# Branch c's finish as a pipeline of tiles, its bonus operand made early, and the rounds' keys moved behind chain steps

## What is computed

```python
# six heads of 64 channels, two directions; t = 128 or 1024 tokens
S = S * w + (S @ -kk)[..., None] * (kk * a) + v[..., None] * k_dir      # the scan, with y = S @ r
k_dir = k[:, :, None, :] * (1 + (a - 1) * k_a)                          # per direction
y = head_norm(ys[0] + ys[1], ln_g, 6)                                   # mean and variance over 64 channels
bonus = sum over both directions and 64 channels of (r * k_dir * r_k)
y = (y + bonus * v) * g                                                 # g = sigmoid(dg) @ g2
```

## Time and profile before

| | |
|---|---|
| runs | 2104.83, 2108.36, 2111.37 us; median 2108.36 |
| profiled execution | 2114.14 us, its span 2112.4 us, mean granted TensorE clock 0.937 |
| PE, DVE, ACT, POOL busy | 1875.6, 1004.3, 601.9, 725.7 us |
| recurrence of branch c | about 656 to 1087 us of the span |
| finish of branch c | 1088.5 to 1179.3 us |

### The profile page before, as it was taken

How to read it: one execution, slowest core, us unless ns; L and a number is a source line. 1 busy time by engine, 2 the same in 40 slices (tenths; PEclk the granted TensorE clock), 3 DMA queues, 4 the chain that set the end, 5 groups by cost and what they waited for, 6 DMA issues and landing times. The chain is left out here.

```text
span 2112.4 us, 49389 instructions
## 1 busy us (share of the span) xinstructions
PE 1875.6 (89%) x20834; PEld 1755.2 (83%) x20834; DVE 1004.3 (48%) x1726; ACT 601.9 (28%) x1330; POOL 725.7 (34%) x559
## 2 busy tenths in 40 slices
PE   6599799998996888878754799999999999999998
PEld 3589798877996677767643699999999999999998
DVE  6603753767334455444458636333433343424254
ACT  4413243322125555445420224110101020201034
POOL 3502431444843222222220512443535344343460
PEclk7799898998998999899975799999999999999999
DMA  9555010111110000000010400120111111111122
GB/s 301 191 176 177 21 42 14 25 62 49 40 41 12 4 8 4 3 4 4 4 36 0 140 21 21 30 60 25 55 37 43 50 30 50 30 50 35 48 57 90
DMA packets 148180, 110.31 MB, mean 52 GB/s; under 512 B 13298, under 2 KB 144393, under 8 KB 147757
## 3 DMA queue, kind: packets, MB, share of 16 engines
q1 hardware_dynamic: 148013, 107.83, 16.8%
HBM read 93.17 MB, written 14.55 MB: 51 GB/s over the span
## 5 line engine op out<-in xcount | busy, mean ns | idle before, releaser
L253 PE MATMUL banks<-Z_r 128*128 128x384 f32 x2016 | 350.9, 334 | 0.0
L253 PEld LDWEIGHTS banks<-Z_r 128*128 128x128 f32 x2016 | 349.5, 188 | 0.4 <-issue 0.2
L2669 DVE SCALAR_TENSOR_TENSOR XT<-banks,MOD,XT 128x128 f32 x224 | 110.8, 516 | 226.1 <-PE banks L253 225.3
L3003 ACT ACTIVATE PAD<-banks 128x384 f32<-128x384 f32 x96 | 47.2, 491 | 504.3 <-PE banks L2898 504.1
L3119 DVE TENSOR_TENSOR PAD<-PAD 128x384 f32<-128x384 f32 x96 | 97.1, 1011 | 144.0 <-ACT PAD L3003 143.9
L235 POOL TENSOR_TENSOR Z_r<-Z,ones 128x512 fp32r<-128x512 f32 x56 | 77.0, 1375 | 253.9 <-DMA Z<-in_mlp_w 253.9
L235 POOL TENSOR_TENSOR W_r<-Z,ones 128x1024 fp32r<-128x1024 f32 x32 | 77.4, 2420 | 241.0 <-DMA Z<-in_mlp_w 240.9
L2898 PE MATMUL banks<-HT_r,W_r 128*128 128x384 f32 x768 | 149.1, 335 | 2.4 <-ACT HT_r L2970 1.6
L2898 PE MATMUL banks<-YT_r,W_r 128*128 128x384 f32 x768 | 148.6, 334 | 0.0
L2898 PE MATMUL banks<-HT_r,Z_r 128*128 128x384 f32 x768 | 148.6, 334 | 0.0
L2898 PEld LDWEIGHTS banks<-HT_r,W_r 128*128 128x128 f32 x768 | 134.4, 188 | 3.3 <-issue 1.9
(11 more groups left out here) (414 smaller groups left out, 4027.4 us busy)
## 6 DMA issues: line engine op xcount, KB each, us to landing
Z<-in_w_mod SPq DMA_DIRECT2D x16, 1024.0 KB, 5.1
Z<-in_mlp_w SPq DMA_DIRECT2D x32, 512.0 KB, 4.3
Z<-in_mlp_w SPq DMA_DIRECT2D x58, 256.0 KB, 2.8
YT<-in_w_in SPq DMA_DIRECT2D x18, 512.0 KB, 3.9
XT<-in_w_mod SPq DMA_DIRECT2D x8, 1024.0 KB, 9.0
residual<-Z SPq DMA_DIRECT2D x1, 4608.0 KB, 18.1
low_part<-XT_r SPq DMA_DIRECT2D x1, 4608.0 KB, 15.9
XT<-low_part SPq DMA_DIRECT2D x8, 576.0 KB, 5.5
```

The costliest lines, as they stand in the source:

```text
L253: mm = nc.tensor.matmul(self.bank(slot, g), w[slot][:, k, :], x(k, g), start=(n == 0 and k == 0), stop=(n == 2 and k == self.blocks - 1))
L2669: ins = nc.vector.scalar_tensor_tensor(out=x, in0=S.PS[3 * slot + g][:, a:b], scalar=S.MOD[:, ds(col, 1), c:c + 1].rearrange("p a b -> p ( ...
L3003: nc.scalar.activation(R[slot][:, grp(g)], up.bank(slot, g), ACT.Relu).then_inc(up.drained[g].sem, 1)
```

## The change

In the rounds: ACT copies q and u of the first half step before `ka_act`; DVE's `k_rows_dve` comes after the zero level's masks; POOL adds the unit matrix first, waits for the state of the first half step, and only then makes `k_dir` and the seeds; the state's multiplication is one instruction over both directions, for which the end decays of the backward direction are stored in reverse order. From round n = 5 on POOL makes the bonus operand of tiles whose keys are no longer needed, in place (in the gate sums and in rows 3 to 5 of Z), six instructions a tile, each followed by a wait for itself: tile 0, then two tiles a round.

In the finish, all written out without a loop: DVE centres tile t, multiplies v by the bonus of tile t - 1, reduces the squares of tile t and completes tile t - 2; ACT squares; POOL divides by the deviation (and does the weights' divisions behind tiles 1, 4 and 7); PE makes the gates for three tiles at a time in three banks, the bonus from the operand that is there, and the transposition. v is overwritten in place. The old body of `finish_c`, quoted above, goes.

```diff
@@ -2240,13 +2243,14 @@
     def round_act(act, chain, nxt, after, par):
         r, n, a = chain, nxt, after
+        if r is not None:
+            q_act(act, r, 0)
+            u_act(act, r, 0)
         if n is not None:
             tok = direction_tiles(act, n)[0]
             for d in range(2):
                 ka_act(act, n, d, tok[d])
         if r is not None:
-            q_act(act, r, 0)
-            u_act(act, r, 0)
             q_act(act, r, 1)
             u_act(act, r, 1)
         for d in range(2):
@@ -2313,10 +2317,9 @@
         heads = lambda x: x.rearrange("p d q n -> p (d q) n")
         nc.vector.tensor_tensor(heads(C.S), heads(C.S), by_block(bank(6)), ALU.add).then_inc(f["added"].sem, 1)
         done(dve, "added", r, j + 1)
-        for d in range(2):
-            ins = nc.vector.tensor_tensor(C.S[:, d, :, :], C.S[:, d, :, :],
-                                          C.ends[par][:, d, :, chunk(d, j)].unsqueeze(2).to_broadcast([P, NP, N]), ALU.mult)
-        ins.then_inc(f["new_state"].sem, 1)
+        ends = C.ends[par].rearrange("p d q j -> p (d q) j")[:, :, j]
+        nc.vector.tensor_tensor(heads(C.S), heads(C.S), ends.unsqueeze(2).to_broadcast([P, 2 * NP, N]),
+                                ALU.mult).then_inc(f["new_state"].sem, 1)
         if between:
             between()
         if j:
@@ -2362,8 +2365,6 @@
                 done(dve, "gram_l", n, d + 1)
                 nc.vector.tensor_tensor(C.LP[:, d, :, :, :].rearrange("p c q n -> p (c q) n"), by_block(bank(d)),
                                         mask(d, LEVELS, 2 * NP), ALU.mult).then_inc(f["masked_l"].sem, 1)
-            for d in range(2):
-                k_rows_dve(dve, n, d)
         if r is not None:
             state_dve(dve, r, par, 0, tiles, first if n is not None else None)
         elif n is not None:
@@ -2371,6 +2372,8 @@
         if n is not None:
             zm_dve(dve, n, 0, 0)
             zm_dve(dve, n, 0, 1)
+            for d in range(2):
+                k_rows_dve(dve, n, d)
         if r is not None:
             state_dve(dve, r, par, 1, tiles)
         if n is not None:
@@ -2408,19 +2411,37 @@
     def r_rows_pool(pool, a, d, par, tok):
         end = N if d == 0 else 0
         done(pool, "exped", a, d + 1)
-        nc.gpsimd.tensor_copy(C.ends[par][:, d, :, :], C.EP[:, d, :, :, end]).then_inc(f["ends"].sem, 1)
+        ends = C.EP[:, d, :, :, end]
+        nc.gpsimd.tensor_copy(C.ends[par][:, d, :, :], ends[:, :, ::-1] if d else ends).then_inc(f["ends"].sem, 1)
         for p in range(NP):
             ins = nc.gpsimd.tensor_tensor(tile_cols(C.RR[par][:, d, :, :], p),
                                           S.Z[:, p, ds(tok, P)].rearrange("p (c n) -> p c n", n=N),
                                           C.EP[:, d, p, :, own(d)], ALU.mult)
         ins.then_inc(f["r_rows"].sem, 1)
+    def bonus_pool(pool, t):
+        at = slice(t * P, (t + 1) * P)
+        both, keys = C.A[:, 0, :, at], S.Z[:, 3:6, at]
+        b = S.bonus_made
+        nonlocal n_bonus
+        def one(ins):
+            nonlocal n_bonus
+            n_bonus += 1
+            ins.then_inc(b.sem, 1)
+            pool.wait_ge(b.sem, b.at(0, n_bonus))
+        one(nc.gpsimd.tensor_tensor(both, both, C.A[:, 1, :, at], ALU.add))
+        for p in range(NP):
+            one(nc.gpsimd.tensor_scalar(both[:, p, :], both[:, p, :], C.bonus_scale[:, p:p + 1], C.bonus_shift[:, p:p + 1],
+                                        ALU.mult, ALU.add))
+        one(nc.gpsimd.tensor_tensor(keys, keys, both, ALU.mult))
+        one(nc.gpsimd.tensor_tensor(keys, keys, S.Z[:, 0:3, at], ALU.mult))
     def round_pool(pool, chain, nxt, after, par):
         r, n, a = chain, nxt, after
         if n is not None:
-            tok = direction_tiles(pool, n)[0]
-            for d in range(2):
-                k_dir_pool(pool, n, d, tok[d])
             for d in range(2):
                 done(pool, "masked_l", n, d + 1)
                 nc.gpsimd.tensor_tensor(C.LP[:, d, :, :, :].rearrange("p c q n -> p (c q) n"),
@@ -2429,6 +2450,12 @@
                                             f["unit_l"].sem, 1)
             before(pool, "tz", n)
             done(pool, "unit_l", n, 2)
+            if r is not None:
+                done(pool, "new_state", r, 1)
+            tok = direction_tiles(pool, n)[0]
+            for d in range(2):
+                k_dir_pool(pool, n, d, tok[d])
+            done(pool, "k_dir", n, 2)
             for d in range(2):
                 for h in range(2):
                     x = rows_of(h)
@@ -2437,6 +2464,15 @@
                                             C.LP[x, d, :, :, :].rearrange("p c q n -> p (c q) n"), m, ALU.mult).then_inc(
                                                 f["seeded"].sem, 1)
                     done(pool, "seeded", n, 2 * d + h + 1)
+        if n == NT // 2 + 1:
+            bonus_pool(pool, 0)
+        if n is not None and n > NT // 2 + 1:
+            for t in (n - 1, NT - n + 1):
+                bonus_pool(pool, t)
+        if n is None:
+            done(pool, "copied", r, 6)
+            for t in (r, NT - r):
+                bonus_pool(pool, t)
         if a is not None:
             tok = direction_tiles(pool, a)[0]
             if r is not None:
...
+            nc.vector.tensor_tensor(C.bonus_scale, S.param("rwkv_k_a"), S.param("rwkv_r_k"), ALU.mult)
+            nc.vector.scalar_tensor_tensor(out=C.bonus_shift, in0=C.one_ka[:, :], scalar=2.0, in1=S.param("rwkv_r_k"),
+                                           op0=ALU.mult, op1=ALU.mult)
...
     scratch = Area(S.XT[:, :, :].rearrange("p k t -> p (k t)")[:, 2 * NP * T:])
+    DEV, YN = ([scratch.cut(2, NP, N) for _ in range(2)] for _ in range(2))
+    STAT = [scratch.cut(3, H) for _ in range(2)]
     G2 = Area(S.PAD[0][:, :]).cut(C_W)
+    heads = lambda x: x.rearrange("p c q n -> p (c q) n")
+    names = ("mean", "centred", "squared", "variance", "log", "rstd", "normed", "bonus", "bonus_v", "turned", "normed_v",
+             "stored")
     f = {k: S.flag("cf_" + k) for k in names}
+    gated, loaded = S.flag("cf_gate"), S.flag("cf_g2", 16)
+    lng = PROWS["rwkv_ln_g"][0]
+    b_bonus, b_turn = S.PS[6], S.PS[7]
...
+            def divide(t):
+                wait(pool, "rstd", t)
+                nc.gpsimd.tensor_tensor(heads(YN[t % 2]), heads(DEV[t % 2]),
+                                        STAT[t % 2][:, 2, :].unsqueeze(2).to_broadcast([P, H, N]), ALU.mult).then_inc(
+                    f["normed"].sem, 1)
+            for t in range(NT):
+                divide(t)
+                if t in (1, 4, 7):
+                    tail.divide(pool, t // 3)
         @block.tensor
         def _(pe):
+            def gates(g):
+                if g >= 2:
+                    wait(pe, "stored", 3 * (g - 1) - 1)
+                for p in range(NP):
+                    mm = nc.tensor.matmul(S.PS[3 * (g % 2) + p][:, 0:GRP], G2[:, p * P:(p + 1) * P],
+                                          S.Z[:, 11, g * GRP:(g + 1) * GRP], start=True, stop=True)
+                mm.then_inc(gated.sem, 1)
+            def bonus(t):
+                wait(pe, "bonus_v", t - 1)
+                nc.tensor.matmul(by_pair(b_bonus), S.halves[:, :], S.Z[:, 3:6, tile(t)], start=True, stop=True).then_inc(
+                    f["bonus"].sem, 1)
+            def turn(t):
+                wait(pe, "normed", t)
+                wait(pe, "normed_v", t - 1)
+                for p in range(NP):
+                    for c in range(2):
+                        for h in range(2):
+                            r = slice(N * h, N * h + N)
+                            mm = nc.tensor.matmul(b_turn[N - N * h:P - N * h, p * P + c * N:p * P + (c + 1) * N],
+                                                  YN[t % 2][r, c, p, :], S.ident[r, N * h:N * h + N], start=True, stop=True)
+                mm.then_inc(f["turned"].sem, 1)
+            bonus(0)
             pe.wait_ge(loaded.sem, loaded.at())
+            gates(0)
+            for t in range(NT):
+                if t:
+                    bonus(t)
+                turn(t)
+                if t in (1, 4):
+                    gates(t // 3 + 1)
         @block.scalar
         def _(act):
             act.preload_act_table_set(EXP_LN)
+            for t in range(NT):
+                wait(act, "centred", t)
+                wait(act, "turned", t - 2)
+                nc.scalar.activation(heads(YN[t % 2]), heads(DEV[t % 2]), ACT.Square).then_inc(f["squared"].sem, 1)
+                wait(act, "variance", t)
+                st = STAT[t % 2]
+                nc.scalar.activation(st[:, 2, :], st[:, 1, :], ACT.Ln, bias=S.eps[:, 1:2], scale=1.0 / N).then_inc(
+                    f["log"].sem, 1)
+                wait(act, "log", t)
+                nc.scalar.activation(st[:, 2, :], st[:, 2, :], ACT.Exp, scale=-0.5).then_inc(f["rstd"].sem, 1)
         @block.vector
         def _(dve):
+            def centre(t):
```

(62 more changed lines are left out.)

80 lines of the change are left out of this document (3 added, 77 removed).

## The result

The changed kernel takes 2055.7 us (median of four runs, 2049.5 to 2062.2) against 2106.6 of the kernel before in the same session: ratio 0.9755, interval 0.9728 to 0.9781, some 51 us faster. The forecast was 2064 (2048 to 2079), 44 us faster. The profiled execution took 2056.4 us around a span of 2054.7.

A forecast was written before the change was run, and what follows sets the result against it. The finish was taken as DVE's and a round as a chain through PE, ACT and DVE; after the change PE's loop paces the finish. Finish 39 plus rounds 5 gave 44 us, from 2108.4 to 2064, range 2048 to 2079.

The forecast's parts named there:

- The finish: Finish of branch c: paced by a loop through PE's queue, ending near 1140 instead of 1179.3, saving 39 us.
- The period of 4.5: Finish, per tile: PE's loop of turn, bonus and DVE's part, 3.9 us at 2.4 GHz, 5.1 at 1.2; 4.5 taken.
- rival B: PE's loop in the finish runs cold and the seeding costs its upper end: 33 us gained, 2075; chance 0.18.
- The collisions of the centring: Finish: DVE's centring grows when it meets POOL's divisions, about four times; 0 to 5 us, 1 taken.
- ka behind the q copy: Rounds: ACT's q copy no longer waits behind ka_act; 0.88 us in seven rounds, 6.2 us gained.
- state multiplication with POOL quiet: Rounds, first halves: one multiplication at 0.55 replaces pairs that met POOL's seeding; 10.0 us gained.
- seeding after new_state: Rounds: k_dir and seeds come later, stalling PE's inversion 0.9 us a round; 7.2 us lost, bounds 0 to 1.6 a round.
- bonus operand against the multiplication: Rounds: POOL's bonus operand overlaps five state multiplications, 0.78 us each; 3.9 us lost.
- A: Rounds give their whole gain and PE stays at full clock in the finish: 57 us, so 2051; chance 0.12.
- C: Finish bound by DVE alone, period 3.72 us: 45 us there, with 5 from the rounds 2058; chance 0.12.
- D: Slower: bonus operand on POOL delays the round; from 3.0 us per tensor_scalar, at 5 us each 2155; chance 0.03.
- E: Order changes but nothing comes of it, each step waiting for what it did before: 2108; chance 0.03.

The follow-up runs named there:

- ka_first: Changed kernel with ACT's ka_act back at the head of the round, ahead of the first q and u copies; 2065.2 us, ratio 0.9810.
- seeds_first: Changed kernel with POOL's four inversion seedings ahead of k_dir, both still behind new_state; 2057.6 us, ratio 0.9749.
- no_bonus_operand: Changed kernel without POOL making the bonus operand, so its bonus output means nothing; 2053.7 us, ratio 0.9742.
- finish_alone: Changed kernel with the old order of the rounds, keeping the new finish and POOL's bonus operand; 2067.8 us, ratio 0.9799.
- changed_again: The changed kernel unchanged, run again in another session; 2064.7 us, ratio 0.9778.
- rounds_alone: Changed kernel with the old finish and without the bonus operand on POOL, only the rounds' edits kept; 2097.2 us, ratio 0.9932.
- two_products: Changed kernel with the state multiplication again in two instructions, one per direction; 2065.3 us, ratio 0.9783.
- keys_unwaited: Changed kernel without POOL's wait for new_state before k_dir and the seeding; 2054.0 us, ratio 0.9744.
- both_moves: Changed kernel with PE's bonus one tile ahead of the transposition and without POOL's wait for new_state; 2046.5 us, ratio 0.9711.

## Why the prediction was right, step by step

**The finish: right, by its own loop.** Forecast 51.2 us in four pieces, measured 49.4 (1073.11 to 1122.52). To the end of tile 0's multiply-adds 11.3, measured 10.1 (1083.17 - 1073.11). Tile 1: 7.5, measured 5.7, because PE was at the full clock for gates and bonus (2.20 and 0.81 us) where I had put a mixed one. To tile 7 with gates(2): 30.0, measured 30.4. The end: 2.4, measured 3.2, the last turn at the low clock (1.55).
- The period of 4.5 was a mean of 3.9 and 5.1. Periods at either end occur: 3.73 at full clock, 4.64 and 5.35 where the bonus took 1.65 us. (The last but one, 3.72, has a bonus of 1.35 us, but also a reduction less.) So rival B's cold loop was real for two tiles, not for all.
- The collisions of the centring, "0 to 5, I take 1": two centrings took 2.34 us and one 1.09 (the L2683 rows above), but only that of tile 8, at 1111.30 (period 5.34 instead of 3.73), was late for PE: 1.6 us. The one at 1094.56 was hidden by PE's slow bonus, which ended at 1096.75.
- Three gates at full clock were put at 1.9 us "by the same rows", which give no such number; they took 2.20. In the steady loop the prediction had 3.9 us at full clock and 3.73 was measured.
- POOL's division took 0.83 us where 1.0 was taken. POOL's timeline as a weight's division meets the stage:
```profile
1093.36 0.83 POOL L2617 TENSOR_TENSOR XT<-XT 128x384 f32<-128x384 f32 x1 [3.81 <-ACT XT L2674]
1094.14 2.35 POOL L2765 TENSOR_TENSOR W_r<-Z,ones 128x1024 fp32r<-128x1024 f32 x1
```
The weight divisions' first instruction starts at 1094.14 and ends at 1096.49; the centring that began at 1094.56 ended at 1096.90, 0.41 us after it. The second case gives the same (POOL's instruction ended 1113.22, the centring 1113.64), and so does the 1.09 us one, which met a tile's division (1084.94 and 1085.35). The Trainium skill (SBUF — State Buffer, SBUF: two separate sides) describes the pair of ports shared by GpSimd and VectorE as an exclusive lock held for a whole instruction, not as a split of the bandwidth; by that rule the centring waits for POOL's current instruction and then runs. The traces agree but for the tail: 0.41 us are left behind POOL's end, where a centring alone takes 0.56. The products from a bank beside the same work kept their 0.54 us.

**The rounds: the sign right, the size too small.** Step by step, in PE's waits over eight rounds:

| step of the prediction | forecast gain | measured |
|---|---|---|
| ka behind the q copy | 6.2 | 5.6 (10.2 to 4.6; back with `ka_first`) |
| state multiplication with POOL quiet | 10.0 | 8.8 (19.9 to 11.1) |
| seeding after new_state | -7.2 | -7.5 as a wait, about -1 in effect (`seeds_first`) |
| bonus operand against the multiplication | -3.9 | 0 (`no_bonus_operand`) |
| PE's gaps of no cause | none | 2.4 (14.0 to 11.6) |
| sum | 5 | 9.4, with 0.1 of small ones |

(That the 19.9 us of PE's waits equal DVE's busy time in the earlier trace rows is chance.) What was mis-sized is the charge against the gain. The collision of 3.9 us was counted in full for five multiplications; three grew, by 1.8 us together and all in second halves, where PE's sum of waits does not show them. Without this term the forecast is 9 us, and the waits give 9.4. And the stall was taken as 0.9 a round on the path; its lower bound in the prediction, "0, if PE's later gaps absorb it", was the better value: without the stall 6.5 of its 7.5 us come back as gaps and other waits. So leaving the stall away would not have brought the full 16 us. Why those gaps are there, and why they are shorter behind a wait, no run shows.

The other 7 us of the rounds' 16.4 belong to no step: PE needed 7.2 us less for the same instructions at the clock of that execution. `finish_alone` shows as much without the new order, and `changed_again` lacks it (288.6 us busy). By times the order is worth 14 us (8 to 20, `rounds_alone`), by stages at equal clock 11 to 13, by PE's waits 9 to 10.

**The mechanism under the 10 us** was half right. POOL quiet during the multiplication is the gain; but the joined multiplication has next to no part in it (`two_products`), and POOL's new wait isn't needed for it, since ACT's late ka does nearly as much (`keys_unwaited`: 12.2 us of waits against 11.1).

**The rivals.** A (rounds at full gain, finish at full clock) was right in its first half at most (14 us by the times, 9.4 by the waits); the granted clock of the finish is 0.74. B and C are answered above: B for two tiles, C only once the bonus stands ahead of the turn. That the changed kernel has a period of 3.73 us at full clock, the number of C, is chance: DVE idles 0.30 us in it behind PE's bonus (row 1108.43). D fell with one row, the group of POOL's tensor_scalar, at 0.47 us each where 0.45 was taken and 3 would have been needed; so a tile's operand is not a microsecond shorter either, as the prediction's other reckoning had it. E fell with the result.
```profile
L2437 POOL TENSOR_SCALAR XT<-XT,misc 128x128 f32<-128x128 f32 x27 | 12.6, 468 | 2.7
```
**The total.** 44 us forecast, 51 measured (46 to 57 from the interval of the ratio), with the same kernel at 47 (`changed_again`, 40 to 54) in another session. The times of forecast and result lie 8.3 us apart, those of the changed kernel's two sessions 9.0. So the total can't confirm the forecast's finer sums; its stages do, the finish within 2.4 us. Both stages gained more than forecast, so the total is not right by errors that cancel.

## What to carry to other kernels

Before a pipeline is charged to an engine's busy time, draw the loop through the in-order queues: in this finish the order of two products in PE's queue was worth about 7 us of 49, of which up to 2 may be PE's clock. When a stall is added to or taken from an engine, read its sum of waits and not one wait: here 6.5 of 7.5 us turned up again, most of them as gaps that the profile gives no cause for. And when several moves of a change protect the same instruction, test each alone: here joining the two multiplications added 0.2 us, and POOL's wait 1.1 beside the late ka.

## What the runs showed that I had not expected

- PE's gaps named "issue" over the eight rounds were 14.0 and 16.6 us in the old order, 10.7 to 12.4 with the seeding wait and 16.2 to 18.1 without it (`seeds_first`, `keys_unwaited`, `both_moves`), while all waits together stayed within 58.2 to 59.9 us in every kernel of the new order but `ka_first`.
- The same 10212 PE instructions took from 278.0 us (granted clock 0.99, `no_bonus_operand`) to 290.6 us (0.94, before). That alone is over 12 us between profiles, more than most steps of this change.
- POOL's division by the deviation, a 128x384 tensor by a factor of 128x6 spread over its blocks, took 0.83 us in seven of nine tiles, against 0.99 for the product of two full tensors.
